# Rows of the next block gathered under the second projection, and y copied by two engines, in a mixture-of-experts block

## The reference, cut to what matters

```python
logits = xt @ w_router + b_router             # xt: (256, 1024), 32 experts
top_v, top_i = lax.top_k(logits, 4)
gates = softmax(top_v)
# for each expert e, on the rows that chose it:
gu  = xblk @ w_gate_up[e] + b_gate_up[e]      # 1024 -> 2048
act = min(gu[:, :1024], 7) * sigmoid(1.702 * ...) * (clip(gu[:, 1024:], -7, 7) + 1)
y   = act @ w_down[e] + b_down[e]             # 1024 -> 1024
out[token] += gate * y
```

## Time and profile before

| | |
|---|---|
| median of 3 runs | 1191.23 us (1187.77 to 1194.48) |
| the profiled execution, its own time | 1186.76 us |
| its span in the profile | 1184.5 us |
| mean granted TensorE clock | 0.938 |
| TensorE busy (matmuls) | 1029.1 us, 87% |
| VectorE, ScalarE busy | 294.9 us (25%), 179.7 us (15%) |
| read from HBM | 462.5 MB, 392 GB/s over the span |
| chain that ended last | TensorE 64%, DMA 23%, VectorE 5% |

### The profile page before, as it was taken

One profiled execution on the slowest core, in us unless ns is written; L12 is line 12 of the kernel. 1 busy time (PEld: TensorE's weight loads), 2 busy tenths in 40 slices (PEclk: granted clock), 3 DMA queues, 4 the chain that ended last, 5 costly groups with the idle time before them and its releaser, 6 DMA issues.

```text
span 1184.5 us, 21565 instructions
## 1 busy us (share of the span) xinstructions
PE 1029.1 (87%) x8299; PEld 502.1 (42%) x8301; DVE 294.9 (25%) x813; ACT 179.7 (15%) x453; POOL 31.6 (3%) x54
## 2 busy tenths in 40 slices
PE   4999999977786999899989998999898989696966
PEld 4847887443342343334333433343334333232323
DVE  4636664241110121111211221112112211111112
ACT  3213340221110111101111111111111111010012
POOL 1001002110000000000000000000000000000000
PEclk9999999978897999899989998999899989898988
DMA  9899825989999979999999999999999999999996
GB/s 351 321 385 380 338 103 226 422 347 417 424 426 423 411 307 425 424 425 396 427 424 425 425 425 427 425 415 425 425 428 411 426 425 424 425 427 427 426 424 261
DMA packets 61484, 464.91 MB, mean 392 GB/s; under 512 B 5900, under 2 KB 10060, under 8 KB 28568
## 3 DMA queue, kind: packets, MB, share of 16 engines
q1 hardware_dynamic: 60736, 462.47, 94.6%
q0 software_dynamic: 336, 1.07, 0.3%
q10 hardware_dynamic: 392, 1.09, 0.2%
HBM read 462.50 MB, written 2.11 MB: 392 GB/s over the span
## 4 chain that ended last, share of the span: by engine, by line
PE 64%; DMA 23%; DVE 5%; issue 4%; ACT 2%; SPq 2%; DVEq 0%; POOL 0%; ACTq 0%
PE pp L1539 23%; DMA arena<-in_w_down_dram 20%; PE pp L1568 13%; PE pp L1325 5%; PE pp L1503 5%; PE pp L1247 2%; PE pp L1338 2%; PE po L1400 2%; PE pp L1257 2%; PE pp L1512 2%; PE po L1484 2%; DMA gain<-gain_dram 2%; DMA arena<-in_w_ada_dram 1%; PE pp L1518 1%; ACT work L720 1%
## 5 line engine op out<-in xcount | busy, mean ns | idle before, releaser
L1539 PE MATMUL pp<-arena,work 128*32 128x256 f32 (+1 forms) x3840 | 379.0, 449 | 20.1 <-ACT work L720 20.1
L1539 PEld LDWEIGHTS pp<-arena,work 128*32 128x32 f32 (+1 forms) x3840 | 168.3, 118 | 214.9 <-issue 131.3
L1568 PE MATMUL pp<-arena,work 128*32 128x256 f32 (+1 forms) x1920 | 200.2, 462 | 54.6 <-DMA arena<-in_w_down_dram 54.6
L1568 PEld LDWEIGHTS pp<-arena,work 128*32 128x32 f32 (+1 forms) x1920 | 77.1, 122 | 157.3 <-issue 67.9
L1091 DVE TENSOR_SCALAR work<-pp 128x128 f32<-128x128 f32 (+1 forms) x74 | 25.0, 338 | 410.2 <-PE pp L1539 410.2
L1503 PE MATMUL pp<-h_sb,work 128*32 128x256 f32 (+1 forms) x480 | 70.0, 514 | 41.9 <-issue 37.5
L723 ACT ACTIVATE work<-work 128x128 f32<-128x128 f32 (+1 forms) x74 | 25.9, 350 | 407.9 <-DVE work L1091 407.9
L1085 DVE COPY work<-pp 128x256 f32<-128x256 f32 (+1 forms) x37 | 19.5, 526 | 250.0 <-PE pp L1503 250.0
L1484 PE MATMUL po<-work 64*128 64x512 f32 x304 | 75.5, 615 | 1.2 <-ACT work L739 1.2
L1503 PEld LDWEIGHTS pp<-h_sb,work 128*32 128x32 f32 (+1 forms) x480 | 22.5, 129 | 84.9 <-issue 79.5
L1325 PE MATMUL pp<-arena 128*128 128x256 f32 x256 | 57.1, 382 | 0.0
(11 more groups left out here) (224 smaller groups left out, 622.7 us busy)
## 6 DMA issues: line engine op xcount, KB each, us to landing
arena<-in_w_gate_up_dram SPq DMA_DIRECT2D x128, 2048.0 KB, 27.7
arena<-in_w_down_dram SPq DMA_DIRECT2D x32, 2048.0 KB, 33.3
arena<-in_w_down_dram SPq DMA_DIRECT2D x64, 1024.0 KB, 20.1
arena<-in_w_ada_dram SPq DMA_DIRECT2D x11, 2048.0 KB, 14.0
arena<-in_w_in_dram SPq DMA_DIRECT2D x4, 2048.0 KB, 19.2
arena<-in_w_gate_dram SPq DMA_DIRECT2D x4, 2048.0 KB, 13.0
arena<-in_w_out_dram SPq DMA_DIRECT2D x2, 2048.0 KB, 10.6
arena<-in_w_ada_dram SPq DMA_DIRECT2D x2, 1024.0 KB, 13.3
```

Of the source, the lines that this page charges most:

```text
L1539: mm = t_.matmul(pp[j * m:(j + 1) * m, UP[hh], 0:w].rearrange("p (s f) -> p s f", s=2), hgT[:, at:at + m], gu_w[slot][:, k, :, r * PAIR:(r ...
L1568: mm = t_.matmul(pp[j * m:(j + 1) * m, UP[0], 0:w], actT[:, at:at + m], wd[:, j * w:(j + 1) * w], start=(n == 0), stop=(n == KD - 1))
```

## The change

It does three things in the experts' loops.

- **The rows of the next block are gathered one block ahead.** `gather(it + 1)` stands inside the second projection of block `it`, ahead of its step n=4, and `turn_rows(it + 1)` behind its last step. The gather always has two column tiles of 512 columns, and the turn four transposes and a copy of 512 columns, in narrow blocks too. VectorE makes `sel` and `selg` for block it+1 once the gate matrix of block `it` is transposed, and copies the rows to `hg` then; ScalarE copies `hgT` at the end of a block. To know where the next block belongs, TensorE loads the next place's two table entries in every block, ahead of step n=4 (`next_place`), and no longer at a place's start; VectorE loads the next expert's number in every block. The first block's rows are gathered before the loop, into the bank `UP[1]`, and for that VectorE makes `rank` and the first `sel` ahead of the block counts (`nblk_i`), where `rank` came last before.
- **The combine is split two and two**: (t=0; j=0, 1) at the start of a block, (t=1; j=0, 1) behind the first projection.
- **y is copied by halves of the partitions**, the lower half by ScalarE, the upper by VectorE (`s_ysv`).

The core of the diff, TensorE's part:

```diff
+            def gather(it, bank):
+                pe.wait_ge(s_sel, it)
                 for t in range(TT):
                     for j in range(2):
+                        mm = t_.matmul(pp[j * TB:(j + 1) * TB, bank, :], sel[:, t, :], h_sb[:, t, j * 512:(j + 1) * 512],
+                                       start=(t == 0), stop=(t == TT - 1))
+                mm.then_inc(s_hg, 1)
+
+            def turn_rows(it):
+                pe.wait_ge(s_hgs, it)
+                for i in range(4):
+                    mm = t_.transpose(pp[:, TURN, i * P:(i + 1) * P],
+                                      hg[:, i // 2 * PAIR + i % 2:(i // 2 + 1) * PAIR:2], ident[:])
+                mm.then_inc(s_turn, 1)
+
+            gather(1, UP[1])
+            pe.wait_ge(s_ysb, 2)
+            turn_rows(1)
...
+            def combine(it, parts, last=False):
+
+                pe.wait_ge(s_ysv, it)
+                pe.wait_ge(s_ysb, it + 1)
+                for t, j in parts:
...
                 pe.wait_ge(s_bgu[slot], landed * 2)
-                pe.wait_ge(s_sel, it)
-                for t in range(TT):
+                combine(it, ((0, 0), (0, 1)))
...
-                combine(it)
+                combine(it, ((1, 0), (1, 1)))
                 turn_half(0)
                 turn_half(1)
...
                 for n, k in enumerate(order):
+                    if n == 2:
+                        pe.wait_ge(s_aTev, halves[1])
+                    if n == 4:
+                        next_place()
+                        pe.wait_ge(s_selTev, it)
+                        gather(it + 1, TOKS)
                     if k in (4, 6):
                         pe.wait_ge(s_dhi[k // 2 - 2], dhi_landed)
...
                 mm.then_inc(s_y, 1)
+                turn_rows(it + 1)
```

On VectorE and ScalarE:

```diff
+                dve.wait_ge(s_selT, it + 1)
+                select_rows(iota[:, bass.ds(next_b * TB, TB)], bass.ds(next_e, 1))
+                select_gates(iota[:, bass.ds(next_b * TB, TB)], bass.ds(next_e, 1))
+                take_rows(it + 1, TOKS)
+                dve.wait_ge(s_y, it)
+                if m == TB:
+                    v.tensor_copy(y_sb[TB:P, :], pp[TB:P, UP[0], :]).then_inc(s_ysv, 1)
+                else:
+                    v.tensor_copy(y_sb[2 * m:3 * m, 0:w], pp[2 * m:3 * m, UP[0], 0:w])
+                    v.tensor_copy(y_sb[2 * m:3 * m, w:2 * w], pp[3 * m:P, UP[0], 0:w]).then_inc(s_ysv, 1)
...
-                    a.copy(y_sb[:, 0:w], pp[:, UP[0], 0:w])
-                    a.copy(y_sb[0:m, w:2 * w], pp[m:2 * m, UP[0], 0:w])
-                    a.copy(y_sb[2 * m:3 * m, w:2 * w], pp[3 * m:P, UP[0], 0:w]).then_inc(s_ysb, 1)
+                        a.copy(y_sb[0:TB, :], pp[0:TB, UP[0], :]).then_inc(s_ysb, 1)
+                    else:
+                        a.copy(y_sb[0:m, 0:w], pp[0:m, UP[0], 0:w])
+                        a.copy(y_sb[0:m, w:2 * w], pp[m:2 * m, UP[0], 0:w]).then_inc(s_ysb, 1)
+                    act.wait_ge(s_turn, it + 1)
+                    a.copy(hgT, pp[:, TURN, :]).then_inc(s_turned, 1)
```

More of the change, by code:

```diff
@@ L1057, in _, with select_rows, select_gates, take_rows @@
             dve.wait_ge(s_const, 7)
+            link(v.scalar_tensor_tensor(out=rank[:], in0=pp[:, 2, RANK:COUNT].rearrange("p (t e) -> p t e", t=TT),
+                                        scalar=1.0, in1=chosen, op0=ALU.add, op1=ALU.mult))
+            link(v.tensor_scalar(rank[:], rank[:], -1.0, None, ALU.add))
+            def select_rows(places, e):
+                for t in range(TT):
+                    ins = v.tensor_scalar(sel[:, t, :], places, rank[:, t, e], None, ALU.is_equal)
+                ins.then_inc(s_sel, 1)
+            def select_gates(places, e):
+                for t in range(TT):
+                    for c in range(2):
+                        ins = v.tensor_scalar(selg[:, t, c, :], places, rank[:, t, e], gate_tab[:, t, e], ALU.is_equal,
+                                              ALU.mult)
+                ins.then_inc(s_selg, 1)
+            def take_rows(it, bank):
+                dve.wait_ge(s_hg, it)
+                v.tensor_copy(hg, pp[:, bank, :]).then_inc(s_hgs, 1)
+            first = slice(0, 1)
+            select_rows(iota[:, 0:TB], first)
             counts = pp[:, 2, COUNT:COUNT + NEXP].rearrange("p (e a) -> p e a", a=1).to_broadcast([P, NEXP, 8])
@@ L1069, in _ @@
             v.scalar_tensor_tensor(out=key, in0=pp[0:NEXP, 2, COUNT:COUNT + NEXP], scalar=float(NEXP), in1=key_add,
[L1070 to L1074, removed]
+                                   op0=ALU.mult, op1=ALU.add).then_inc(s_tabs, 1)
+            take_rows(1, UP[1])
+            select_gates(iota[:, 0:TB], first)
             item = dve.alloc_register("dve_item")
@@ L1098, in block_of, with blocks @@
                     v.tensor_tensor(x_sig, x_lin, x_sig, ALU.mult).then_inc(s_actv, 1)
-            def select(places, e):
-                dve.wait_ge(s_tabs, 1)
-                for t in range(TT):
-                    ins = v.tensor_scalar(sel[:, t, :], places, rank[:, t, e], None, ALU.is_equal)
-                ins.then_inc(s_sel, 1)
-                for t in range(TT):
-                    for c in range(2):
-                        ins = v.tensor_scalar(selg[:, t, c, :], places, rank[:, t, e], gate_tab[:, t, e], ALU.is_equal,
-                                              ALU.mult)
-                ins.then_inc(s_selg, 1)
-            def blocks(nb, wide, e):
+                dve.wait_ge(s_selT, it + 1)
[8 more added lines that the diff above has]
+                    v.tensor_copy(y_sb[2 * m:3 * m, w:2 * w], pp[3 * m:P, UP[0], 0:w]).then_inc(s_ysv, 1)
+            def blocks(nb, wide, n):
                 with dve.Fori(0, nb) as b:
@@ L1144, in _ @@
             with dve.Fori(1, NEXP) as n:
-                nb, wide, e = place_of(bass.ds(n, 1))
-                blocks(nb, wide, bass.ds(e, 1))
+                nb, wide = place_of(bass.ds(n, 1))
+                blocks(nb, wide, n)
             dve.wait_ge(s_x1b, 16)
@@ L1497, in block_of @@
                 pe.wait_ge(s_bgu[slot], landed * 2)
[L1498 to L1499 removed]
+                combine(it, ((0, 0), (0, 1)))
+                for hh in range(2):
                     for j in range(tiles):
[L1501 to L1509 removed]
                         rows = bias_rows_of(slot, hh)
```

80 lines of the change are left out of this document (33 added, 47 removed).

## The result

| | before | after |
|---|---|---|
| median | 1187.89 us (20 runs, 1184.70 to 1194.48) | 1194.18 us (20 runs, 1188.57 to 1199.12) |
| ratio to before, 95% interval | | 1.0045 (1.0033 to 1.0058) |
| the profiled execution, its own time | 1186.76 us | 1194.74 us |
| its span | 1184.5 us | 1192.5 us |
| TensorE busy | 1029.1 us | 1048.8 us |

The changed kernel is 0.45% slower (0.53% by the two medians alone), where +0.4% was forecast, and the interval lies on both sides of the bound of 0.5%. That the sum came out near the truth is partly luck: single terms were off by 3 to 4 us, in both directions.

A forecast was written before the change was run, and what follows sets the result against it. The memory stream bounds the kernel; TensorE delays cost only where the queue runs empty and at the end. 2.3 - 0.3 + 1.4 + 0 + 1 = +4.4 us: 1191.2 profiled, 1195.6 on the median's scale, range 1187 to 1206.

The forecast's parts named there:

- Narrow second projection: Second projection of a narrow block: gather (1.76) and register-load bubble (0.8) added to 3.6 us, +2.6.
- Crossing a border: Narrow block, from a second projection to the next first projection across a place's border: 4.16 us becomes 2.4, -1.7.
- Wide blocks: Wide block: second projection +1.76, start in the same expert -1.3, between the projections 0; total +0.5 us.
- Behind a long wait: From the w_down wait's end to the first projection, at half clock: -2.5 us, bounds -1 and -3.3.
- The start: Place 0, narrow: `s_dhi_free` reached 2.3 us later, ends 0 and +4; first gather's move counted 0 (-2 to +1.5).
- Place 5: Place with two wide blocks where the queue runs empty: `s_dhi_free` shifts by -0.3 us, ends -3 and +2.
- Place 9: Place with a wide and a narrow block: `s_dhi_free` shifts by +1.4 us, ends -1.5 and +3.5.
- Places 13, 17, 21: The same 1.4 us shift lies under the 1.6 to 2.2 in hand: 0, ends 0 and +1.5 each.
- The end: Kernel's end: TensorE's +0.6 counts in full, ScalarE copies `hgT` once more; +1 us, ends -0.5 and +2.5.
- Rival 1: Stream dries out in the large experts, three more gaps at places 13 to 21: about +12 us, 1203, chance 0.28.
- Rival 3: Register loads inside the blocks are hidden: +2.0 us, 1193, chance 0.12.
- Rivals 2 and 4: First: the stream's gaps close, -6 us, 1185, chance 0.12. Second: the queue hides all shifts, 0, 1191, chance 0.08.

The follow-up runs named there:

- e4: Changed kernel with the two register loads ahead of the loop moved above the first block's turn; 0.9988 of the kernel before.
- e8: Kernel before with only the combine split, one half ahead of the bias, the other behind the first projection; 1.0031 of the kernel before.
- e1: Changed kernel with every gather inside the second projection computed twice; 1.0188 of the kernel before.
- e3: Changed kernel with the combine unsplit, all four matmuls behind the first projection; 0.9994 of the kernel before.
- e7: Changed kernel with y copied by ScalarE alone, as before the change; 1.0042 of the kernel before.
- e11: Changed kernel with the combine whole behind the first projection and the first register loads above the first turn; 0.9977 of the kernel before.
- e10: e4 with six linked memsets on VectorE ahead of place 0 as a pure delay; 1.0041 of the kernel before.
- e5: The changed kernel itself, unaltered, measured and profiled once more; 1.0060 of the kernel before.

## Why the prediction was right, and where it was not

The forecast was +4.4 us for the profiled execution; it came to 8.0 there, and to 6.3 between the medians. By its steps, each taken from the profiles:

- **Narrow second projection, +2.6.** It went from 3.59 us to 6.06 (544.54 to 550.60): +2.47. Right as a sum, with both parts off: the gather takes 1.94 us instead of 1.76, and the bubble at the loads is 0.35 and not 0.8. I had carried the 0.8 over from the earlier trace rows, where the loads stood behind the end of a block and a branch. The Trainium skill, "TensorE: Matmul & The Clock Gate", section "Architectural detail: the array is 16× 32×32, not 1× 128×128", has a queue of 64 instructions, by which the bubble would be nothing (an estimate); the trace, with 0.35, puts it between.
- **Crossing a border, -1.7.** Measured 2.87 us for 4.16: -1.3. The step that took 2.4 us left out 0.23 of issue ahead of the combine and took 0.96 for 1.13.
- **Between the projections, -0.3.** Measured 9.80 us for 10.52 from start to start: -0.7. In all a narrow block costs +0.5, where +0.6 was forecast.
- **Wide blocks, +0.5.** The second projection 8.77 us (425.19 to 433.96) for 7.02, with no bubble, as forecast. The start in the same expert 3.10 us for 4.12 (-1.0 instead of -1.3), between the projections -0.1: +0.6.
- **Behind a long wait, -2.5.** At place 5 it is 7.14 us to the first projection, and 7 were forecast; but I had taken the 9.3 of place 17 for both, and place 5 itself took 8.75 before (366.18 to 374.93), so this saved 1.6 and not 2.5. At place 17 it is 4.3 us, from T = 739.04 to 743.36, for 9.3: -5.0, outside the bound of -3.3. TensorE's timeline there:

```profile
732.77 1.94 PE L1499 MATMUL pp<-h_sb,work 128*64 128x512 f32 x8 [0.32 <-issue]
736.57 1.07 PE L1593 MATMUL pp<-arena,work 128*32 128x256 f32 x16 [1.86 <-DMA arena<-in_w_down_dram]
739.04 1.07 PE L1593 MATMUL pp<-arena,work 128*32 128x256 f32 x16 [1.40 <-DMA arena<-in_w_down_dram]
...
741.28 1.13 PE L1522 MATMUL po<-work 64*128 64x512 f32 x4 [0.50 <-DVE work L1126]
```

  The half combine runs at full clock (1.13; at place 5, at half clock, 2.08). The gather now stands in the wait itself, and the clock had not fallen when the wait ended, where before it had (3.68). The bound assumed half clock on both sides. That the gather in the wait kept the clock up is not shown: at place 13 it stands there too, between idles of 0.32, 1.98 and 0.87 us, and the clock fell all the same (617.5 us; 6.0 us to the first projection).
- **The start, +2.3: the step that failed.** 5.2 us. The term that I set at 0, "no row decides", measured +2.75: the first projection starts 8.96 us behind M for 6.21. The chain has 2.00 us of it as the register loads, and e4 took 1.9 of them away. The order of the instructions showed them behind the turn; I priced the loads inside the blocks and forgot the pair ahead of the loop. My upper end of +1.5 covered the gather, the tables and the block counts, but not them. The half combine of place 0, 2.08 us at half clock, was not in the term either; e8 shows it alone (+2.1 to the first projection). Without the loads the first projection begins 6.74 us behind M in e4, some 0.5 to 0.8 later than before (the play of M), within the bounds. The rest of the block, +2.46, is the forecast 2.3.
- **Place 5, -0.3.** +3.5, of which the late clock is nearly all: with an early one the same loop takes 59.4 us (e4), and 60.1 before, so -0.7. This was in none of the steps, since I took the length of half clock from one place of one kernel.
- **Place 9, +1.4.** Slice 18 is full (424), nothing lost: -2.0 instead of +1.4, for the same reason as place 17.
- **Places 13, 17, 21: 0.** Right: from place 13's issue to place 17's are 119.5 us in both kernels. (From 9 to 13 it is 117.3 before and 119.6 after, since place 9's own issue came late before.) By the prediction's own working the issue of place 17 now comes 4.4 us ahead of the computed end of the queue (T = 739.0, issue at 788.95), for 4.5 before: what the second projections added came back behind T.
- **The end, +1.** +2.8, above the upper end of 2.5. From L480 to the first projection are 3.64 us for 2.79 (half a combine at half clock, 2.08, stands in it), from there to the final combine 18.59 for 16.84 (the two inner steps of above, +1.75). In e4 the clock is back ahead of this projection, and L480 to the end is 30.4: so the late clock costs some 2.3 us, and the change without it +0.5. The kernel before lost 1.5 us in the same projection too (9.02 for 7.46), but its chain goes through gain2, which lands at 1175.6, about when TensorE's last combine ends (1176.3): there the loss was covered, here nothing covers it.

Rival 1's gaps came in e1, in a kernel whose TensorE is the bound there, but not in the changed kernel. Rival 3, hidden loads, is nearly what happened inside the blocks (0.35 us of bubble). Rivals 2 and 4 fell with slices 8 and 14.

Of the three parts of the change, the split costs (e8, without a late clock at place 5; e3), the copies by halves gain nothing (e7), and the gather one block ahead, with the combine whole and the register loads moved, brings about 0.2% (e11, 0.9977, the interval ends below 1). Why the clock came back late at place 5 stays open beyond what e10 shows: the instant at which the work falls can decide it.

## What to carry to other kernels

Read the straight code ahead of a loop in the order of its instructions as carefully as the loop: a register load behind the last wait of a prologue is idle time of the bound engine. Half of a computation moved from a covered stretch to an uncovered one costs what it takes there (0.92) and gives back only what the old cover left open (0.58). And where an engine's clock falls in waits, compare an edit of a few microseconds also with its own shift: give the same kernel a harmless delay, and see whether the difference stays.

## What the runs showed of the hardware

- How long TensorE stays at half clock behind a wait is not a constant. It was busy with hardly a gap from the end of the wait ahead of place 5, and the full clock came back about 4 us later in e4 and nearly 13 us later in after, e5, e7 and e10; in e3 and e11 it took 9 us. The two profiles of one kernel (after, e5) agree, and a shift of 2 us of the same loop decides it (e4 against e10). What it depends on beyond the timing stays open.
- Its price in this kernel is about 3 us in a wide first projection where nothing covers it (15.8 us for 13.05), and 1.5 in a narrow one (9.0 for 7.5).
- Two register loads of TensorE's sequencer in the middle of a narrow second projection leave 0.35 us of bubble; ahead of a place whose queue is empty, 2.0 us.
